# Windowed attention in a hybrid trunk: both key/value heads at once

## The reference

```python
s_loc = jnp.einsum('bqhgd,bkhd->bhgqk', qi, ki).astype(F32) * scale
s_loc = jnp.where(valid, s_loc, -jnp.inf)
s_ctx = jnp.einsum('bqhgd,bchd->bhgqc', qi, kc).astype(F32) * scale
p = jax.nn.softmax(jnp.concatenate([s_loc, s_ctx, sink_l], axis=-1), axis=-1).astype(v.dtype)
return (jnp.einsum('bhgqk,bkhd->bqhgd', p[..., :3 * BLOCK], vi)
        + jnp.einsum('bhgqc,bchd->bqhgd', p[..., 3 * BLOCK:-1], vc))
```

## Time and profile before

| | us |
|---|---|
| median of 3 runs | 1971.47 (1967.23 to 1972.42) |
| the profiled execution | 1968.78 |
| its span, first to last instruction | 1967.0 |
| attention stretch, layer 0 | 158.46 |
| attention stretch, layer 1 | 121.90 |
| PE busy in the span | 1710.1 (87%) |

### The profile page before, as it was taken

The page is one execution under the profiler, slowest core; times in us unless marked ns, Lnnn a source line. Parts: engine busy times, 40 slices in busy tenths (PEclk is TensorE's granted clock), DMA queues, the critical chain, the costliest instruction groups (busy, mean ns, idle before and its releaser), DMA issues.

```text
span 1967.0 us, 22403 instructions
## 1 busy us (share of the span) xinstructions
PE 1710.1 (87%) x9042; PEld 1361.6 (69%) x9042; DVE 758.0 (39%) x1220; ACT 524.7 (27%) x837; POOL 559.8 (28%) x252
## 2 busy tenths in 40 slices
PE   4789985777969999999999987995779689999997
PEld 2567764444857888888888876775556577878785
DVE  3441153554372222222222365525553723332425
ACT  3212123454223111111111122333443332222222
POOL 0612133000244233223322213235001553443431
PEclk8789997899989999999999996897799889999998
DMA  6534530000053222233333110221000312313121
GB/s 236 174 109 142 155 108 1 1 1 1 22 171 105 88 85 72 101 107 107 107 107 107 43 43 22 64 64 43 0 1 22 107 65 76 116 64 128 64 86 43
DMA packets 122190, 155.17 MB, mean 79 GB/s; under 512 B 20352, under 2 KB 89872, under 8 KB 122128
## 3 DMA queue, kind: packets, MB, share of 16 engines
q1 hardware_dynamic: 122128, 154.32, 24.3%
HBM read 152.21 MB, written 2.10 MB: 78 GB/s over the span
## 4 chain that ended last, share of the span: by engine, by line
PE 74%; DVE 12%; ACT 7%; issue 2%; SPq 2%; POOL 1%; DMA 1%; DVEq 0%; ACTq 0%; POOLq 0%
PE ps L1389 15%; PE ps L1390 15%; PE ps L1391 15%; PE ps L1650 5%; PE ps L1651 5%; PE ps L1652 5%; PE ps L1600 2%; ACT s_at L746 2%; PE ps L1329 2%; ACT pT L519 1%; DVE hl L1268 1%; PE ps L1574 1%; DVE s_at L1197 1%; PE ps L1671 1%; PE ps L1672 1%
## 5 line engine op out<-in xcount | busy, mean ns | idle before, releaser
L413 POOL TENSOR_TENSOR wl<-raw,wh 128x1024 fp32r<-128x1024 f32 x144 | 353.9, 2471 | 1041.2 <-ACT wh L519 1041.2
L1389 PE MATMUL ps<-zh,wh 128*128 128x512 f32 x1632 | 592.7, 363 | 37.8 <-DVE zl L979 16.7
L1390 PE MATMUL ps<-zl,wh 128*128 128x512 f32 x1632 | 587.3, 360 | 0.0
L1391 PE MATMUL ps<-zh,wl 128*128 128x512 f32 x1632 | 583.5, 358 | 0.0
L1389 PEld LDWEIGHTS ps<-zh,wh 128*128 128x128 f32 x1632 | 314.6, 193 | 122.2 <-issue 49.4
L1391 PEld LDWEIGHTS ps<-zh,wl 128*128 128x128 f32 x1632 | 314.0, 192 | 46.4
L1390 PEld LDWEIGHTS ps<-zl,wh 128*128 128x128 f32 x1632 | 315.0, 193 | 43.4
L519 ACT ACTIVATE wh<-raw 128x1024 fp32r<-128x1024 f32 x144 | 148.7, 1058 | 399.9 <-PE ps L1391 290.7
L1281 DVE SCALAR_TENSOR_TENSOR xT<-ps,modcol,xT 128x512 f32<-128x512 f32 (+1 forms) x264 | 169.2, 661 | 104.1 <-PE ps L1652 100.4
L1262 DVE TENSOR_TENSOR hf<-gs,ps 128x512 f32<-128x512 f32 x66 | 37.6, 597 | 403.4 <-ACT gs L790 403.3
L1650 PE MATMUL ps<-hh,wh_d 128*128 128x512 f32 x480 | 173.4, 361 | 11.4 <-DVE xT L1281 11.4
(11 more groups left out here) (220 smaller groups left out, 1777.8 us busy)
## 6 DMA issues: line engine op xcount, KB each, us to landing
raw<-in_w_gate_dram SPq DMA_DIRECT2D x22, 1024.0 KB, 7.0
raw<-in_w_up_dram SPq DMA_DIRECT2D x22, 1024.0 KB, 9.4
raw_m<-in_w_mod_dram SPq DMA_DIRECT2D x22, 1024.0 KB, 5.2
raw_d<-in_w_down_dram SPq DMA_DIRECT2D x20, 1024.0 KB, 5.0
raw<-in_w_in_dram SPq DMA_DIRECT2D x14, 1024.0 KB, 5.4
raw<-in_w_mod_dram SPq DMA_DIRECT2D x11, 1024.0 KB, 5.3
raw_n<-in_w_mod_dram SPq DMA_DIRECT2D x9, 1024.0 KB, 5.2
raw<-in_w_out_dram SPq DMA_DIRECT2D x32, 256.0 KB, 4.4
```

The costliest lines, as they stand in the source:

```text
L413: nc.gpsimd.tensor_tensor(dst, src, hi.bitcast(F32), ALU.subtract).then_inc(sem(done), 1)
L1389: MM(dst, wt_h[:, h, w], zh[:, k, c0:c1], start=(k == 0), stop=False)
L1390: MM(dst, wt_h[:, h, w], zl[:, k, c0:c1], start=False, stop=False)
L1391: last = MM(dst, wt_l[:, h, w], zh[:, k, c0:c1], start=False, stop=(k == KC - 1))
```

## The change

The attention is numbered by blocks `n` over both layers (0 to 5, 6 to 9), and both key/value heads of a block go together.

- The keys lie once (`akh`, `akl`: 128 rows), the zero fills go. A score product uses 64 rows: head 0 in rows 0 to 63, head 1 in rows 64 to 127, issued in turn, head 0 into banks 0 and 1, head 1 into banks 2 and 3. The pair of a next `c` waits for both masks of this one.
- DVE's mask multiplies by the negated scale and takes the minimum with the negated sink (`nsink`, one small operation at the start), so that the result is the exponential's bias as it stands; ACT computes exp(-x + bias). The sink's exponential comes last.
- The weights are not divided. The transposes of head 0 are copied to `pT` by ACT, those of head 1 by DVE; tile `kk` is transposed when both copies of tile `kk - 1` are made. `pT` is a ring of seven.
- The value products of both heads follow each other, in column halves of the array.
- New: eight small products spread the reciprocals of the sums over rows (`inverse_rows`, column halves), ACT copies them to `modrow`, DVE multiplies the output by them (`normed`) into `oat`, ACT copies its high part, POOL subtracts for the low part.
- The order is written anew in all four programs: the tiles of block `n - 1` between the score groups of block `n`. The group norm's buffers `oc` and `gsq` move to the unused end of `wh[1]` and `wl[1]`, since `s_at` is twice as large.

The core of the diff; removed functions are those printed above:

```diff
--- before.py
+++ after.py
+        _, _, _, oc, _, _, _, gsq, _ = overlay([
+            ("raw_o", [P, 2, 2048], F32), ("wh0_o", [P, 2048], F32), ("wh1_o", [P, NT], F32), ("oc", [P, NT], F32),
+            ("wh1_p", [P, 512], F32), ("wl0_o", [P, 2048], F32), ("wl1_o", [P, NT], F32), ("gsq", [P, NT], F32),
+            ("wl1_p", [P, 512], F32)])
...
-        akh, akl = (t[1][:, :, :].rearrange("p h n -> p (h n)")[:, 0:2 * NT].rearrange("p (g n) -> p g n", g=2)
-                    for t in (wh, wl))
-        s_at, pT = overlay([("s_at", [P, 2, 4, 640], F32), ("pT", [P, 5, SX], F32)],
-                           under=[(n + "_a", s, d) for n, s, d in attn_base])
+        akh, akl = (t[1][:, :, :].rearrange("p h n -> p (h n)")[:, 0:NT] for t in (wh, wl))
+        s_at, pT, _, oat = overlay([("s_at", [P, 2, 8, 640], F32), ("pT", [P, 7, SX], F32), ("osb_a", [P, 2, NT], F32),
+                                    ("oat", [P, SX], F32)], under=[(n + "_a", s, d) for n, s, d in attn_base])
...
+        def rb_slot(n):
+            return 2 * tiles_before(n + 1) + n
+        def slot_of(n, kk, kv):
+            return 2 * (tiles_before(n) + kk) + n + kv
...
                 pool.wait_ge(sem("loA"), 2 * A_OUT[l] + 2)
-                for kv in range(2):
-                    pool.wait_ge(sem(f"qk_hi{l}"), kv + 1)
-                    rows, rest = slice(HD * kv, HD * kv + HD), slice(HD - HD * kv, P - HD * kv)
-                    zeros = blk[rest, HD * kv:HD * kv + HD].unsqueeze(1).to_broadcast([HD, NT // HD, HD])
-                    for t in (akh, akl):
-                        ch.link(nc.gpsimd.tensor_tensor(t[rest, kv, :].rearrange("p (a n) -> p a n", n=HD), zeros, zeros,
-                                                        ALU.subtract))
-                    lo(akl[rows, kv, :], ak[rows, :], akh[rows, kv, :], f"qk_lo{l}")
-                    pool.wait_ge(sem(f"qk_lo{l}"), kv + 1)
+                pool.wait_ge(sem(f"qk_hi{l}"), 1)
+                lo(akl, ak[:, :], akh, f"qk_lo{l}")
                 for q in range(4):
                     W = NT if l == 0 else SX
-                    pool.wait_ge(sem(f"qk_hi{l}"), 3 + q)
+                    pool.wait_ge(sem(f"qk_hi{l}"), 2 + q)
                     lo(aql[:, q, 0:W], aq[:, q, 0:W], aqh[:, q, 0:W], f"qk_lo{l}")
+                for n in range(ATT_AT[l], ATT_AT[l + 1]):
+                    q = slice(P * ATT[n][1], P * ATT[n][1] + P)
+                    pool.wait_ge(sem("at_f"), n + 1)
+                    pool.wait_ge(sem("at_hi"), n + 1)
+                    lo(zl[:, 2:6, q], oat[:, :].rearrange("p (c q) -> p c q", c=4), zh[:, 2:6, q], "at_lo")
...
+                def exps(n, c):
+                    wd = P * len(tiles(n))
+                    for kv in range(2):
+                        hd = 4 * kv + c
+                        act.wait_ge(sem("at_max"), 8 * n + 2 * c + kv + 1)
+                        nc.scalar.activation(s_at[:, n % 2, hd, 0:wd], s_at[:, n % 2, hd, 0:wd], ACT.Exp,
+                                             bias=stats[:, n % 2, hd:hd + 1], scale=-1.0,
+                                             accum_out=stats[:, n % 2, 24 + hd:25 + hd])
+                def sink_exp(n):
+                    act.wait_ge(sem("at_nb"), n + 1)
+                    nc.scalar.activation(stats[:, n % 2, 16:24], stats[:, n % 2, 8:16], ACT.Exp).then_inc(sem("at_exp"), 1)
+                def transposed(n, kk):
+                    if n < ATT_AT[l] or kk >= len(tiles(n)):
+                        return
+                    g, q = slot_of(n, kk, 0), 2 * (tiles_before(n) + kk)
+                    act.wait_ge(sem("at_tr"), q + 1)
+                    if q >= N_PT:
+                        act.wait_ge(sem("at_mm"), (q - N_PT) // 2 + 1)
+                    copy(pT[:, q % N_PT, :], ps[:, 5 + g % 2, :]).then_inc(sem("at_pa"), 1)
+                def inverse_rows(n):
+                    if n < ATT_AT[l]:
+                        return
+                    act.wait_ge(sem("at_rb"), n + 1)
+                    if n:
+                        act.wait_ge(sem("at_f"), n)
+                    copy(modrow[:, :], ps[:, 5 + rb_slot(n) % 2, :]).then_inc(sem("at_rc"), 1)
+                def att_hi(n):
+                    if n < ATT_AT[l]:
+                        return
+                    q = slice(P * ATT[n][1], P * ATT[n][1] + P)
+                    act.wait_ge(sem("at_f"), n + 1)
+                    copy(zh[:, 2:6, q], oat[:, :].rearrange("p (c q) -> p c q", c=4)).then_inc(sem("at_hi"), 1)
+                for n in range(ATT_AT[l], ATT_AT[l + 1]):
+                    j = n - ATT_AT[l]
+                    exps(n, 0)
+                    att_hi(n - 2)
+                    gn_square(j)
+                    exps(n, 1)
+                    transposed(n - 1, 0)
+                    transposed(n - 1, 1)
+                    exps(n, 2)
+                    gn_root(j)
+                    transposed(n - 1, 2)
+                    transposed(n - 1, 3)
+                    exps(n, 3)
+                    sink_exp(n)
+                    transposed(n - 1, 4)
+                    inverse_rows(n - 1)
+                    gn_hi(j)
+                last = ATT_AT[l + 1] - 1
+                att_hi(last - 1)
+                for kk in range(5):
+                    transposed(last, kk)
+                inverse_rows(last)
+                att_hi(last)
...
+                def masked(n, c):
+                    i = ATT[n][1]
+                    wd = P * len(tiles(n))
+                    nl = wd - SC
                     mask = {0: S_MASK + P, 3: S_MASK3}.get(i, S_MASK if i < 4 else S_MASK + 384)
+                    dve.wait_ge(sem("at_sc"), 4 * n + c + 1)
+                    for kv in range(2):
                         hd = 4 * kv + c
+                        pair = ps[:, 2 * kv:2 * kv + 2, :].rearrange("p b n -> p (b n)")
+                        V.tensor_tensor_reduce(s_at[:, n % 2, hd, 0:wd], pair[:, SX - nl:SX + SC], K[:, mask:mask + wd], -SCALE,
+                                               nsink[:, 8 * l + hd:8 * l + hd + 1], ALU.add, ALU.min,
+                                               stats[:, n % 2, hd:hd + 1]).then_inc(sem("at_max"), 1)
+                def sink_arg(n):
+                    dve.wait_ge(sem("at_max"), 8 * n + 8)
+                    V.tensor_tensor(stats[:, n % 2, 8:16], sinkb[:, 8 * l:8 * l + 8], stats[:, n % 2, 0:8], ALU.add
+                                    ).then_inc(sem("at_nb"), 1)
+                def inverse(n):
+                    if n < ATT_AT[l]:
+                        return
+                    dve.wait_ge(sem("at_exp"), n + 1)
+                    ch.link(V.tensor_tensor(stats[:, n % 2, 24:32], stats[:, n % 2, 24:32], stats[:, n % 2, 16:24], ALU.add))
+                    V.reciprocal(stats[:, n % 2, 24:32], stats[:, n % 2, 24:32]).then_inc(sem("at_rs"), 1)
+                def transposed(n, kk):
+                    if n < ATT_AT[l] or kk >= len(tiles(n)):
+                        return
+                    g, q = slot_of(n, kk, 1), 2 * (tiles_before(n) + kk) + 1
+                    dve.wait_ge(sem("at_tr"), q + 1)
+                    if q >= N_PT:
+                        dve.wait_ge(sem("at_mm"), (q - N_PT) // 2 + 1)
+                    V.tensor_copy(pT[:, q % N_PT, :], ps[:, 5 + g % 2, :]).then_inc(sem("at_pv"), 1)
+                def normed(n):
+                    if n < ATT_AT[l]:
+                        return
+                    dve.wait_ge(sem("at_mm"), tiles_before(n + 1))
+                    dve.wait_ge(sem("at_rc"), n + 1)
+                    if n:
+                        dve.wait_ge(sem("at_lo"), n)
+                    V.tensor_tensor(oat[:, :], ps[:, 7, :], modrow[:, :], ALU.mult).then_inc(sem("at_f"), 1)
+                for n in range(ATT_AT[l], ATT_AT[l + 1]):
+                    j = n - ATT_AT[l]
+                    masked(n, 0)
+                    normed(n - 2)
+                    gn_lo(j - 1)
+                    gn_centre(j)
+                    masked(n, 1)
+                    inverse(n - 1)
+                    transposed(n - 1, 0)
+                    transposed(n - 1, 1)
+                    masked(n, 2)
+                    transposed(n - 1, 2)
+                    transposed(n - 1, 3)
+                    masked(n, 3)
+                    sink_arg(n)
+                    transposed(n - 1, 4)
+                    gn_scale(j)
+                last = ATT_AT[l + 1] - 1
+                normed(last - 1)
+                inverse(last)
+                for kk in range(5):
+                    transposed(last, kk)
+                normed(last)
...
+                def scores(n, c):
+                    i = ATT[n][1]
                     loc = local(i)
                     nl = P * len(loc)
+                    if 8 * n + 2 * c:
+                        pe.wait_ge(sem("at_max"), 8 * n + 2 * c)
+                    q = slice(P * i, P * i + P)
+                    areas = [(1, slice(0, SC), slice(SX, NT))]
```

(74 more changed lines are left out.)

162 lines of the change are left out of this document (19 added, 143 removed).

## The result

The changed kernel takes 1905.8 us (median of four runs, 1904.7 to 1906.8), against 1970.0 for the kernel before (four runs, 1967.2 to 1972.4). The ratio is 0.9674, with a 95% interval of 0.9657 to 0.9691: 64 us, or 3.3%, faster. The sign was right, the gain was forecast at 42.5 us and is half as large again.

A forecast was written before the change was run, and what follows sets the result against it. TensorE was taken to bound the kernel; walking through attention iterations gave 213.9 us at full clock, plus 19.0 clock and 5.0 projection clock: 237.9 against 280.4, a gain of 42.5, so 1926 us, range 1906 to 1957.

The forecast's parts named there:

- three when it stands alone: Attention values: a lone fp32 pair in column halves costs three records, 1.28 us, against two per pair in a run.
- The clock: Attention stretches: TensorE below full clock adds 19 us, the middle of two counts, 15 and 23.
- The second count: Attention: 8 stretches behind long TensorE waits lose some 2.9 us each at half clock, 23 us.
- (2): Attention iteration: TensorE waits 2.9 us behind tile 0's transposes, for both copies of that tile.
- (1): Attention iteration: between score groups 0 and 1 TensorE waits 1.6 us for both of DVE's masks.
- (3): Attention iteration: the inverse rows wait 1.1 us for ACT's last copy, queued behind exponentials.
- The hand-over: Attention to output projection: DVE, ACT and POOL take 3.0 us; half clock behind it adds 5 us over two layers.
- The switch of 0.17 us: Attention: each change between full array, row halves and column halves costs TensorE 0.17 us; 64 more are 11 us.
- A: Attention pairs overlap only partly: score pairs serial, about 1948 us; value and inverse pairs too, 1966; chances 0.15 and 0.04.
- B: Attention clock stays low, so the kernel gets slower: 1975 to 2021 us; chance 0.06.
- C: Attention queues of ACT and DVE hand over worse: 40 tiles with 0.5 us more, about 1945 us; chance 0.13.
- D: Better: attention at full clock throughout or half of that gain, 1902 to 1912 us; chance 0.10.

The follow-up runs named there:

- e2: Changed kernel with head 1's value product left out for all key tiles but each block's first (30 of 40 products): 1909.2 us, ratio 0.9668.
- e5: Changed kernel with 30 of head 1's 40 value products written into head 0's column half: 1924.3 us.
- e7: Changed kernel with the group norm's reciprocals on DVE left out: 1890.2 us.
- e1: Changed kernel with all score passes of head 0 issued before those of head 1, instead of in turn: 1922.7 us.
- e6: Changed kernel with DVE again passing over all eight heads' weights (times 1.0) before each block's transposes, like the old division: 1959.7 us.
- e11: Changed kernel with TensorE's waits filled by unused products, DVE's inverse and last low part rearranged, and the group norm's reciprocal cut into two halves: 1879.1 us.

## Why the prediction was right or wrong

**The bound, the place and the sign: right.** The gain is in the two attention stretches to within the few us that the untouched parts move, it comes from less TensorE work, and nothing else replaced TensorE (DVE is busy for 58% of them). Score starts of consecutive blocks in layer 0's middle lie 25.8 and 24.8 us apart, and some 25 were forecast.

**The step that failed: "three when it stands alone".** The forecast's stretches were 213.9 + 19.0 = 232.9 us, measured were 217.9, 15.0 less. The prediction read rows 7 as fp32 pairs whose second half starts with the first half's second record, so that a lone pair costs three records, 1.28 us. e2 and e5 show that it costs two, 0.85: 0.43 us less for each of 40 tiles is 17 us of work. At the share that e5 gives (17.2 us of time for 25.5 of work) this is 11.5 us of the 15, an estimate. The rows that it rested on were a run of pairs, which can't tell this apart. In rows 7, 4 x 2 x 0.21 + 0.21 = 1.9 came near to 2.08; but full overlap with the 0.17 us of the end of a run, which the prediction had itself read from rows 6, gives 8 x 0.107 + 0.17 = 1.02 for the sixteen records in column halves (0.107 is a quarter of 0.43, for 128 columns instead of 512), and 1.02 is what the row shows. For a run of pairs the price held: the four pairs of the inverse rows took 0.92 us where 1.0 stood.

**The clock: its term is not settled to the microsecond.** The forecast had 0.85 to 0.95, measured were 0.83 and 0.84, so it fell a little further than thought. 19 us was the term; filling the waits gave back 8.8 us of the stretches for 0.10 of the 0.165 lost, some 14 in all if the rest is worth as much. The second count had a slip, half of 5.55 is 2.8 and not 2.9, which moves the 19 by less than 1. The count by "stretches at half clock behind each long wait" was the right mechanism: wait (2) is followed by eight transposes at 1.97 us.

**The waits.** (2), the wait behind the transposes of tile 0, was put at 2.9 and is 2.53 in the iteration shown. (1) was put at 1.6 and is 1.37 in the same iteration, but 5.11 in the first full one: that the masks are queued behind a reciprocal of 3.35 us was in the DVE sum, not in the walk, and e7 prices it at 10 us of the stretches. (3), the inverse rows behind ACT's copy, was put at 1.1 for each iteration and is 0.6 in all ten. These two misses go against each other. The transposes' wait for pT fell to 19.1 us (14.3 + 4.8), where "near 20" stood.

**The hand-over.** 2.86 us measured against 3.0, so the sum of DVE, ACT and POOL was right. What followed was not: half clock was charged at 5 us for two layers and was there in one, for 3.34 us at 0.51, 1.7 us. That is 3.3 more of the miss. Three microseconds of wait were taken to be enough because 4.58 was the earlier trace rows; for no wait between 1.4 and 4.58 had the clock behind it been read. The runs show that such a wait decides nothing by itself (12 of 20), so that one layer and not both lost its clock in this execution is chance as far as is known.

**The other terms.** The switch of 0.17 us holds: a lone pair's 1.01 is 0.85 and 0.16. Between value products and inverse rows, both in column halves, there is next to none: the 0.92 us above are 8 x 0.107 and 0.06. Score groups took 1.09 with the switch, 1.07 was forecast. What was said to cost nothing, POOL's low parts and the start of the kernel, shows nothing outside the stretches (1.0 us in all).

**Added up**, the forecast's span would be 1686.6 outside the stretches + 237.9 = 1924.5; the span was 1903.6, 20.9 less: 15.0 in the stretches (an estimated 11.5 of them the value pairs, 3.5 the inverse rows, waits and clock together, of which the inverse rows are less than 1 and the runs don't divide the rest), 5.0 of the hand-over's clock term that lies outside, and 0.9 by which the time outside fell below that of the kernel before, with the 1.7 us of half clock found there in it.

**The rivals.** A (no or partial overlap) fell with e1 and e5. B (the clock stays low, slower) was near in kind: at 0.74 and 0.71 in e6, nearly all of the gain was gone, through waits (at most 43 us) and through the clock (at least 10). C (worse queues) was there in one place, the reciprocal. D (better, at full clock) has the right time, 1902 to 1912, for the wrong reason: the clock was lower than in the forecast, and the work was less. The range ended at 1906 because D was held to need a better clock. A second way to be better, that the forecast's own price of a pair was too high, had no rival and no share in the range; two records instead of three, with the 11.5 us that this is estimated to be worth, would have moved its end to 1895.

**What was missed about the change itself** is how much hangs on the division. The prediction took DVE's 80 divisions as work beside TensorE's and the walk as given. That the merged order brings little with them in one piece (e6: 53 us) is not a part of the sum that went wrong, since the sum was of the whole; but a reader of the sum alone would take the pairs for the gain.

## What to carry to other kernels

Where products of two heads use half of the array each, issue them pairwise and count a pair as one product, even a pair of fp32 products that stands alone; check with the shortest lone pair that the trace has, not with a run of pairs. When blocks are merged, ask which pass on another engine now has no block beside it, and move that pass to the output, or cut it into pieces that lie between what TensorE waits for (done here for the group norm's reciprocal in e11, not for the division). When TensorE's waits are short but many, look at the granted clock before and after them, and fill them with products that nobody reads: here 252 of them gave 11 us.

## What the runs showed of the hardware

Lone fp32 pairs in different column halves start together (1.08 us for four records against 1.07 for two and 1.93 for four in one half). fp32r products in different row halves run side by side even where all of one half's are issued ahead of the other's: in e1 head 1's first pass starts at 390.32 us and head 0's last at 390.79. A wait of 2.85 to 2.89 us in front of the output projection was followed by a clock below full in 12 of 20 cases and by a full one in 8; the work ahead of it doesn't decide it alone, since layer 0 kept its clock in the changed kernel (1.00) and lost it in e1 (0.83) behind the same last block. A mean clock of 0.83 in the attention became 0.94 with 252 idle products, and 1.00 in layer 1 of e11. A reciprocal on DVE took 3.35 us for 512 columns and 1.74 for 256, five times the 0.68 us of a copy from PSUM over 512 columns.
